# The first output projection and the first gate-and-up pair in the in-place weight slots, as tile pairs with seven products for eight in six of their k pairs

## The reference

```python
mixed = g_a * (y_a @ w_branch_a[l]) + g_b * (y_b @ w_branch_b[l])
h = h + mixed @ w_out[l]                                    # "out": 2048 x 2048
hn = rmsnorm(h, ffn_norm[l])
h = h + (jax.nn.silu(hn @ w_gate[l]) * (hn @ w_up[l])) @ w_down[l]   # 2048 x 5632, 5632 x 2048
```

## Time and profile before

| | us |
|---|---|
| median of 3 runs | 2443.72 (2443.34 to 2443.83) |
| profiled execution | 2443.6 |
| its span | 2441.9 |
| TensorE busy | 2427.4 (99%) |
| VectorE busy | 1805.1 (74%) |
| ScalarE busy | 1369.7 (56%) |

### The profile page before, as it was taken

One profiled execution on the slowest core, in us unless ns is written; L12 is line 12 of the kernel. 1 busy time (PEld: TensorE's weight loads), 2 busy tenths in 40 slices (PEclk: granted clock), 3 DMA queues, 4 the chain that ended last, 5 costly groups with the idle time before them and its releaser, 6 DMA issues.

```text
span 2441.9 us, 28978 instructions
## 1 busy us (share of the span) xinstructions
PE 2427.4 (99%) x11187; PEld 2016.9 (83%) x11187; DVE 1805.1 (74%) x2292; ACT 1369.7 (56%) x1726; POOL 51.3 (2%) x96
## 2 busy tenths in 40 slices
PE   9999999999999999999999999999999999999998
PEld 7888888888888888888888888888788888888887
DVE  6455555655698888989777587664789999998854
ACT  6456556445555555556556464564666666666543
POOL 1000020000000000000001100000000000000000
PEclk9999999999999999999999999999999999999999
DMA  7655655666666666666666545556566666666664
GB/s 231 194 172 155 190 149 164 190 199 203 189 199 196 200 198 199 191 188 208 196 207 202 168 151 163 154 192 194 169 195 196 191 198 190 197 190 193 218 200 156
DMA packets 239587, 460.11 MB, mean 188 GB/s; under 512 B 16614, under 2 KB 18832, under 8 KB 239072
## 3 DMA queue, kind: packets, MB, share of 16 engines
q1 hardware_dynamic: 237744, 452.65, 60.4%
q0 software_dynamic: 1680, 5.69, 0.8%
q10 hardware_dynamic: 32, 0.01, 0.0%
HBM read 456.19 MB, written 2.10 MB: 188 GB/s over the span
## 4 chain that ended last, share of the span: by engine, by line
PE 98%; DVE 1%; ACT 1%; DMA 0%; issue 0%; DVEq 0%; SPq 0%; ACTq 0%
PE acc L686 13%; PE acc L688 13%; PE acc L687 13%; PE acc L988 13%; PE acc L990 13%; PE acc L989 13%; PE mis L988 3%; PE mis L990 3%; PE mis L989 3%; PE acc L707 1%; PE acc L706 1%; PE acc L705 1%; PE mis L659 1%; PE mis L1252 1%; PE mis L784 1%; PE mis L1161 1%
## 5 line engine op out<-in xcount | busy, mean ns | idle before, releaser
L1572 ACT ACTIVATE wf<-wf_raw 128x1024 fp32r<-128x1024 f32 x452 | 471.3, 1057 | 472.5 <-DVE wf_raw L2365 196.3
L2004 DVE TENSOR_TENSOR lo<-raw,hi 128x1024 fp32r<-128x1024 f32 (+1 forms) x405 | 487.8, 1220 | 319.5 <-ACT hi L1307 316.8
L2377 DVE TENSOR_TENSOR wf<-wf_raw,wf 128x1024 fp32r<-128x1024 f32 x452 | 533.4, 1219 | 57.1 <-ACT wf L1572 53.7
L1307 ACT ACTIVATE hi<-raw 128x1024 fp32r<-128x1024 f32 (+1 forms) x405 | 417.5, 1051 | 265.8 <-PE acc L688 211.5
L988 PE MATMUL acc<-wf,xb_hi 128*128 128x512 f32 x874 | 343.1, 393 | 0.0
L990 PE MATMUL acc<-wf,xb_lo 128*128 128x512 f32 x874 | 340.5, 390 | 0.0
L989 PE MATMUL acc<-wf,xb_hi 128*128 128x512 f32 x874 | 340.1, 389 | 0.0
L686 PE MATMUL acc<-hi,xa_hi 128*128 128x512 f32 (+1 forms) x704 | 274.6, 390 | 0.0
L688 PE MATMUL acc<-hi,xa_lo 128*128 128x512 f32 (+1 forms) x704 | 271.7, 386 | 0.0
L687 PE MATMUL acc<-lo,xa_hi 128*128 128x512 f32 (+1 forms) x704 | 271.4, 386 | 0.0
L686 PE MATMUL acc<-hi,xb_hi 128*128 128x512 f32 x608 | 241.3, 397 | 0.0
(11 more groups left out here) (480 smaller groups left out, 3678.7 us busy)
## 6 DMA issues: line engine op xcount, KB each, us to landing
raw<-in_w_in SPq DMA_DIRECT2D x216, 512.0 KB, 4.2
wf_raw<-in_w_ffn_in SPq DMA_DIRECT2D x160, 512.0 KB, 3.7
wf_raw<-in_w_down SPq DMA_DIRECT2D x88, 512.0 KB, 4.2
wf_raw<-in_w_gate SPq DMA_DIRECT2D x80, 512.0 KB, 3.8
wf_raw<-in_w_up SPq DMA_DIRECT2D x80, 512.0 KB, 4.2
wf_raw<-in_w_ffn_out SPq DMA_DIRECT2D x44, 512.0 KB, 3.8
raw<-in_w_ffn_out SPq DMA_DIRECT2D x44, 512.0 KB, 4.8
raw<-in_w_out SPq DMA_DIRECT2D x32, 512.0 KB, 4.7
```

The source lines that it names most:

```text
L1307: nc.scalar.activation(hi[:, slot, :, 0:width], raw[:, slot, :, 0:width], ACT.Copy)\
L1572: nc.scalar.activation(wf[:, f_slot[c], 0, :, :], wf_raw[:, f_slot[c], 1, :, :], ACT.Copy)\
L2004: V.tensor_tensor(lo[:, slot, :, 0:width], raw[:, slot, :, 0:width], hi[:, slot, :, 0:width].bitcast(F32), ALU.subtract).then_inc(lo_ready, 1)
L2377: V.tensor_tensor(wf[:, f_slot[c], 1, :, :], wf_raw[:, f_slot[c], 1, :, :], wf[:, f_slot[c], 0, :, :].bitcast(F32), ALU.subtract).then_inc ...
```

## The change

"out" becomes two pairs of tiles (out pair 0 and 1) and the first gate-and-up tiles become ffn pair 0, all three in the in-place slots, ahead of ffn pair 1. Out pair 0 has forms at k 3 and 5, out pair 1 at 0, 3 and 5, ffn pair 0 at k 5. Ffn pair 1 is no longer the first and gets F_S whole. The activation sums are made twice, from `xa` for "out" and then from `xb`. The residual is loaded whole into `hres` (one load of 2 MB) as soon as the attention is done, and `new_strip` adds to it; `res`, `add`, `keep` and `swiglu` go. The strips 0 and 1 are turned before k 7 of out pair 1, strips 2 and 3 before k 2 of ffn pair 0. The entry from the ring into the slots now lies between the branch tiles and "out".

The diff, cut to its core:

```diff
+O_S = (3, 5)
+X_ORDER = (1, 2, 0)
+E_S = (5,)
...
-            ("gate1", 4, KD, 0), ("branch", 8, 8, 4), ("out", 4, KD, 4), ("ffn", 2 * F_FIRST, KD, FT),
+            ("gate1", 4, KD, 0), ("branch", 8, 8, 4), ("out", 0, KD, 4), ("ffn", 0, KD, FT),
...
+                    elif i == first:
+                        forms = dict(out=O_S, ffn=E_S, ffn2=F_S[1:])[stage]
...
@@ TensorE
             for p in run_b:
                 begun = set()
                 for k in range(p.nk):
-                    if p.stage == "ffn" and k == p.nk - 1:
+                    if p is out0 and k == 1:
+                        pe.wait_ge(side, i1 - 1)
+                        turn(i1 - 1, stg, 0)
+                    if p is out0 and k % 2 == 0:
+                        pe.wait_ge(side, i1 - DT + k // 2 + 1)
+                    if p is out1 and k == p.nk - 1:
+                        pe.wait_ge(y_ok, p.no + 1)
+                        for j in range(2):
+                            turn(i1 + j, strip(j), j)
+                    if p is f0 and k % 2 == 0:
+                        pe.wait_ge(side, i1 + k // 2 + 1)
+                    if p is f0 and k == 2:
+                        for j in range(2):
+                            turn(i1 + 2 + j, strip(2 + j), j)
+                    if p in ffn_b and k == p.nk - 1:
                         pe.wait_ge(y_ok, p.no + 1)
                         turn(i2 + p.i - 1, stg, 1)
@@ ScalarE
+            for k in range(3):
+                f_hi_of(out0, k, 0)
+                f_hi_of(out0, k, 1)
+            side_hi(i1 - 1, xa, 4 * (DT - 1))
+            x_form_hi("out", 1)
+            f_hi_of(out0, 3, 0)
+            f_hi_of(out0, 3, 1)
+            f_hi_of(out0, 4, 0)
+            t_hi_of(out0, 3)
+            x_form_hi("out", 2)
+            f_hi_of(out0, 4, 1)
...
+            x_form_hi("ffn", 2)
+            f_hi_of(f0, 5, 0)
+            f_hi_of(f0, 5, 1)
+            f_hi_of(f0, 6, 0)
+            t_hi_of(f0, 5)
+            h_squares(3)
+            root(2, rs_h)
...
@@ VectorE
+            def to_next(p):
+                after = run_b[p.no + 1]
+                more = sums(after, 0)
+                next(more)
+                middle_end(p)
+                next(more)
+                dve.wait_ge(t4_ok, after.set(0) + 1)
+                f_lo_of(after, 0, 0)
+                f_lo_of(after, 0, 1)
+                f_lo_of(after, 1, 0)
+                t_lo_of(after, 0)
+                finish(p)
+                finish_up(p)
+
+            f_lo_of(out0, 0, 0)
+            f_lo_of(out0, 0, 1)
             results(Count(F_OLD), -1)
+            mix(Count(odd + 2 * (DT - 1)), D + (DT - 1) * W)
+            f_lo_of(out0, 1, 0)
+            f_lo_of(out0, 1, 1)
+            x_forms("out", 1)
+            f_lo_of(out0, 2, 0)
+            f_lo_of(out0, 2, 1)
+            side_lo(i1 - 1, xa, 4 * (DT - 1))
+            x_form_lo("out", 1)
+            strassen(out0, 3)
+            x_forms("out", 2)
+            f_lo_of(out0, 4, 0)
+            f_lo_of(out0, 4, 1)
+            x_form_lo("out", 2)
+            strassen(out0, 5)
+            x_forms("out", 0)
+            f_lo_of(out0, 6, 0)
+            f_lo_of(out0, 6, 1)
+            x_form_lo("out", 0)
+            f_lo_of(out0, 7, 0)
+            f_lo_of(out0, 7, 1)
+            middle(out0)
+            to_next(out0)
...
+            f_lo_of(f0, 2, 0)
+            f_lo_of(f0, 2, 1)
+            f_lo_of(f0, 3, 0)
+            h_lo(2)
+            f_lo_of(f0, 3, 1)
+            h_lo(3)
+            dve.wait_ge(side, i1 + 1)
+            x_forms("ffn", 0)
+            f_lo_of(f0, 4, 0)
+            dve.wait_ge(side, i1 + 2)
+            x_forms("ffn", 1)
+            x_form_lo("ffn", 0)
+            f_lo_of(f0, 4, 1)
+            dve.wait_ge(side, i1 + 3)
+            x_forms("ffn", 2)
+            x_form_lo("ffn", 1)
+            x_form_lo("ffn", 2)
+            strassen(f0, 5)
+            norm4(2, ss_h4, ss_h, rs_h, SQ["h"])
+            for k in (6, 7):
+                f_lo_of(f0, k, 0)
+                f_lo_of(f0, k, 1)
+            middle(f0)
+            to_next(f0)
...
@@ POOL
             pool.wait_ge(y_done, 2 * MH)
-            for j in range(DT):
-                if j:
-                    pool.wait_ge(staged, stages(PH["out"][2] + j - 1) - 1)
-                pool.dma_start(res[:, :, :], a["x"][0].rearrange("(t p) n -> p t n", p=P)[:, :, j * W:(j + 1) * W])\
-                    .then_inc(res_in, 16)
+            pool.dma_start(hres[:, :, :], a["x"][0].rearrange("(t p) n -> p t n", p=P)).then_inc(res_in, 16)
```

More of the change, by code:

```diff
@@ L113, in __init__ @@
         self.c0, self.g0, self.t0, self.par = c0, g0, t0, t0 % 2
-        self.wide = stage in ("ffn", "ffn2")
+        self.wide = stage in ("out", "ffn", "ffn2")
     def chunk(self, k, h):
@@ L510, in old_use, with evictions, forms_due @@
             return max(n for n in range(start - RING, start) if n % RING // 2 == f_slot[c] % 2) + 1
+        def evictions(run, par):
+            n = PH["ffn2"][1] + 2 * F_FIRST if run else PH["out"][1]
+            return 2 * len(range(par, n, 2))
+        def forms_due(stage, q):
+            at = ("out", "ffn", "ffn2").index(stage)
+            return len(F_S) * at + (X_ORDER if stage == "out" else range(len(F_S))).index(q) + 1
         def sums_of(p):
@@ L961, in _ @@
                      hook=None if isinstance(i, int) else {0: lambda: turn(i + (i0 - 1), stg, 0)})
[L963 to L974, removed]
+            i1, i2 = PH["out"][2], PH["ffn"][2]
             bank_p1, bank_q7 = misf[0][:, 0:W], misf[0][:, W:2 * W]
@@ L1021, in operand @@
             def operand(p, kb, t):
-                x = xb if p.wide else [ff_hi, ff_lo]
+                x = xa if p.stage == "out" else xb if p.wide else [ff_hi, ff_lo]
                 return [x[j][:, kb, t * P:(t + 1) * P] for j in range(2)]
@@ L1612, in p1_copy @@
                     act.wait_ge(ff_out, 2 * FT)
-                elif p.stage == "ffn":
+                elif p in ffn_b:
                     act.wait_ge(staged, stages(i2 + p.i - 1))
+                elif p in (out1, f0):
+                    act.wait_ge(staged, stages(i1 + 2 * p.no - 2))
                 elif p is d1:
@@ L2319, in x_forms @@
-            def x_forms(q):
-                k = F_S[q]
+            i1, i2 = PH["out"][2], PH["ffn"][2]
+            def x_forms(stage, q):
+                k, x, n = F_S[q], xa if stage == "out" else xb, forms_due(stage, q)
+                if n > 1:
+                    dve.wait_ge(xf_sum, n - 1)
                 tmp = usum[:, 0, :].rearrange("p (a b) -> p a b", a=2)
-                chain.step(V.tensor_tensor(tmp, xb[0][:, 2 * k:2 * k + 2, :].bitcast(F32),
-                                           xb[1][:, 2 * k:2 * k + 2, :].bitcast(F32), ALU.add))
+                chain.step(V.tensor_tensor(tmp, x[0][:, 2 * k:2 * k + 2, :].bitcast(F32),
+                                           x[1][:, 2 * k:2 * k + 2, :].bitcast(F32), ALU.add))
@@ L2482, in _, with h_lo @@
-            for p in run_b[:n_ffn]:
+            def h_lo(j):
+                side_lo(i1 + j, xb, 4 * j, gains(V_FFN + 4 * j), pair=j % 2)
+            def to_next(p):
[11 more added lines that the diff above has]
+                finish_up(p)
@@ new lines, in _ @@
+            strassen(out1, 3)
+            new_strip(out0, 1)
+            f_lo_of(out1, 4, 0)
+            f_lo_of(out1, 4, 1)
+            strassen(out1, 5)
+            for k in (6, 7):
+                f_lo_of(out1, k, 0)
+                f_lo_of(out1, k, 1)
+            middle(out1)
+            middle_end(out1)
+            f_lo_of(f0, 0, 0)
+            h_lo(0)
+            finish(out1)
+            f_lo_of(f0, 0, 1)
+            finish_up(out1)
+            f_lo_of(f0, 1, 0)
+            h_lo(1)
@@ L2497, in _ @@
                 if after.stage == "ffn":
-                    more = sums(after, 0)
-                    next(more)
-                    middle_end(p)
-                    next(more)
-                    dve.wait_ge(t4_ok, after.set(0) + 1)
-                    f_lo_of(after, 0, 0)
-                    f_lo_of(after, 0, 1)
-                    f_lo_of(after, 1, 0)
-                    t_lo_of(after, 0)
-                    finish(p)
-                    finish_up(p)
+                    to_next(p)
                 else:
```

220 lines of the change are left out of this document (97 added, 123 removed).

## The result

The changed kernel takes 2448.99 us (median of 15 runs, 2448.59 to 2450.64), the kernel before 2443.63 beside it (15 runs, 2442.84 to 2444.19). The ratio is 1.0023, 95% interval 1.0016 to 1.0031: slower by 5.4 us, where 5.2 was forecast. A second measurement gave 1.0025 (1.0015 to 1.0035). The profiled execution took 2449.6, its span 2447.9, which is 6.0 longer than before.

What follows compares the result with a forecast made beforehand. TensorE, busy 99% of the span, bounds the kernel, with VectorE ahead by little. -4.8 - 0.2 + 5.6 (out) + 4.6 (ffn pair 0) = +5.2 on 2443.6 profiled, for a median of 2448.9 us; range 2443.5 to 2452.

Steps and rivals of the forecast that it cites:

- What goes: 21 matmuls fewer (4.76 us) and no 0.2 us wait at the old entry into the in-place slots: 5.0 us less.
- Entry: Start of the in-place slots: VectorE splits a chunk before evicting the accumulator TensorE needs; 1.1 us stall (0.2 to 1.4).
- First out pair: VectorE's queue through out pair 0 into out pair 1 is 5.2 us late; with finish_up 5.6, Entry's 1.1 included.
- T: Moment at which TensorE starts the first output tile, 514.6 us in the kernel before; T+n is n us later.
- The 0.4 for finish_up: In out pair 1, finish and finish_up end after TensorE asks for the second accumulator: 0.4 us more.
- Second out pair, later pairs: In out pair 1 VectorE catches up, no stall; from ffn pair 1 on its idle 4.8 us absorbs what is left.
- rival 2: The lag runs on: ffn pairs 1 and 2 pay 1.5 us each again, 2450.4 to 2451.9 us; chance 0.08.
- ffn pair 0: VectorE late: 2.6 us stall before k 6, then 1.6 and 0.4 (finish_up) at the handover; together 4.6 us.
- The residual: One 2 MB load beside the branch stage in place of four of 512 KB: 0 us, ends 0 and +1.5.
- Rival 3: The 2 MB load starves the branch stage: up to 1.5 us, 2449.5 to 2450.4 us; chance 0.05.
- Rival 1: VectorE's lead absorbs both chains: 2438.7 us, chance 0.07; only one absorbed: 2443.3 or 2444.3 us, chance 0.10.
- Rival 4: Full VectorE latencies between instructions, 0.085 us more on some 90 instructions of both chains: 2456.5 us; chance 0.02.

Runs made afterwards that it cites:

- the last kernel: Changed kernel with eviction first and activation sums moved ahead of VectorE's waits, one ffn copy later on ScalarE: 2439.17 us, ratio 0.9981 against the kernel before.
- the additions: Kernel before, with one, two, three and two VectorE additions of 128x1024 ahead of middle in ffn pairs 3, 5, 7 and 9: 2456.8 us, ratio 1.0053.

## Why the prediction was right

The cause, its places and its size held, with one mechanism missing.

- *What goes.* 21 matmuls, 4.8 us, and 0.2 at the old entry. Shown: the last kernel gets nearly all of it.
- *Entry.* 1.1 forecast, 1.2 measured. Putting the eviction first removes it. (ScalarE's start in rows 5 is 0.26 after TensorE's boundary, not 0.24, which moves nothing.)
- *First out pair.* Forecast 0.5 before k 5, 0.9 before k 6 and 2.7 in k 0 of pair 1. Measured 0.3 (two small ones), 0.8 and 0.3 + 2.0. VectorE was to be done with the handover at T+49.5, and the matmul that waited for it starts at 563.61, T+49.5. The 0.4 for finish_up did not come: TensorE's half clock gave VectorE that time. Where the 2.0 gap had full clock behind it, finish_up cost 0.2. The two short waits of VectorE for ScalarE, priced at 0.63, are there with 0.51 each.
- *Second out pair, later pairs.* No gap, the period stays at 42.4: rival 2 is wrong.
- *ffn pair 0.* 2.6 forecast before k 6, 2.4 measured. The 1.6 + 0.4 at the handover came as 0.2: the eight matmuls at half clock put 1.6 us between the two, so TensorE asked that much later. Here the clock cost nothing, since VectorE set the end. No profile has the gap of 2.4 with full clock behind it, which would show the 1.6.
- *The sum.* Forecast stalls 10.2. Measured gaps 7.1 and half clock 3.2, of which about 1.9 stand in place of forecast stalls (1.6 at T+125; 0.3 at T+50, where the kernel with four loads, at full clock, has its last turn only 1.25 earlier); with the 1.1 of slower first distances behind the gaps the last turn is 6.4 later against T, not 5.2. That T came 0.5 earlier, and that the median lies 0.6 under the profiled execution, brings the median back to the forecast. The agreement to 0.1 us is therefore partly luck; to about 1 us it is not.
- *The residual.* 0, and four loads make no difference. Rival 3 is wrong.
- *Rival 1* is wrong for this order and right for another: in the last kernel the same work is carried, with two of the three sets in VectorE's idle before T. The forecast priced VectorE's queue as the code wrote it, which was right, but took its length (38.6 us and 8.3 for the handover) for the whole matter. Its order against the waits counts as much: with two sets and their splits, 4.8 us, taken out ahead of T, the last gap was still 1.9, and it went when the third set moved a few instructions ahead.
- *Rival 4* is wrong: with distances 0.085 longer for each instruction, the handover would have ended well behind T+49.5.

## What to carry to other kernels

Count an engine's queue in order, from one wait that it must meet to the next; its busy share (37.6 of 42.4 us beside TensorE's 42.4) says nothing of a burst. Work added to the queue is free only ahead of a wait that comes whatever happens (here, for weights whose slot isn't free yet): 2.4 us of it cost nothing there, and 1.9 a few instructions later. And where one engine is busy 99% of the time, price a gap of more than 2 us above its length: every gap of 2.3 and more cost 1.6 to 2.9 on top here, or hid as much of a later wait.

## What the runs showed of the hardware

- TensorE drops to half rate for 5 to 9 matmuls (0.43 apart, 1.6 to 2.9 us more) behind gaps of 2.3 us and longer: at all nine such gaps of the three pairs and of the additions. Behind gaps of 2.0 it did so at three of five, behind 1.9 at none of two, behind 1.4 or less at none, and not behind the 1.7 before the transposes of `hres` (about 1720 us in the changed kernel) either. In the 20 us before each it had been busy but for gaps of at most 0.8. In the changed kernel the drop begins with the fifth matmul after the gap, behind the additions already in the turn. The distance at the lower level, 0.427, is 512 columns at 1.2 GHz; the Trainium skill, "TensorE: Matmul & The Clock Gate", section "Back-to-back issue gap", gives the same.
- GpSimd and VectorE, both with two SBUF inputs, slow each other: a 128x512 sum on VectorE takes 0.94 us for 0.69, and on GpSimd 1.3 to 2.2; a 128x128 subtraction on GpSimd takes 1.32 beside VectorE's splits and 0.46 beside an instruction of VectorE with one input in PSUM.
